# A PEER value stage that takes 32 of its 512 latent tokens by gathered rows, with 16 modulation tiles moved to the input stage

## The chip, the cores and the metric

One core of a Trainium2 chip runs the whole step as one program. The metric is device microseconds of one execution. Times of a kernel are medians of repeated executions; one more execution is taken with the hardware profiler, and all rows below come from that one.

## The reference

Two trunk layers over 128 prompt tokens and 512 latent tokens of 1024 features. Each layer is a mixer and then PEER, a product-key mixture of 16,384 experts. For every token 8 heads pick 16 experts each (128 picks, `idx`) with softmax gates `gsm`. What matters here, cut from the reference:

```
ue = u_tab[idx]
act = jax.nn.gelu(jnp.einsum('td,thkd->thk', xb, ue))
ve = v_tab[idx]
return jnp.einsum('thk,thkd->td', (gsm * act).astype(ve.dtype), ve)
```

The result is multiplied by one of six rows of adaLN modulation and added to the token. That modulation is `silu(c) @ w_mod + b_mod`, 6,144 columns a layer, 48 tiles of 128.

## The kernel before

All data is fp32. A product runs as three fp32r matmuls of split operands (high x high, high x low, low x high), so every weight tile is loaded, split into `w_hi` and `w_lo`, and used three times. Tokens lie in the free dimension as columns 0 to 127 (prompt) and 128 to 639 (latent), features in the partitions.

PEER is dense for the latents. In the **input stage** of a layer, 128 chunks of `u` (128 experts by 1024 features) are multiplied with all tokens: per chunk 24 matmuls of 512 latent columns (`latent_steps`), and per four chunks 24 matmuls for the prompt (`prompt_steps`). ScalarE applies gelu and stores the activations to DRAM (`act_s`). Meanwhile VectorE does the routing (top 16 of keys, then of pairs, `route`), and GpSimd scatters the latents' gates into a zeroed dense table `gate_d`, one indirect DMA for each of 4 tiles x 128 picks (`scatter_gates`). In the **value stage** each of 128 chunks of `v` is multiplied with the product `p` of activations and gates: for a chunk, `form` multiplies a loaded pair `ag` of 512 columns (activations, gates), ScalarE and VectorE split it into `p_his` and `p_los`, `low_v` makes the low part of the weights, and TensorE runs `value_step` for 8 feature tiles (`dt`) with three matmuls each: 24 matmuls of 512 columns a chunk, 3,072 a layer. All 8 sums stay in PSUM over the whole stage, one bank each (`v_bank`). There are 8 slots for weights and for `p`, and 4 for `ag`. Loops run over 16 bodies of 8 chunks.

The prompt's 128 tokens are not dense in the value stage: for pick number k of all 128 tokens, GpSimd gathers 128 rows of `v` (`fetch_row`, 8 buffers `found`) and 128 activations (`fetch_act`), and VectorE adds row times gate times activation to `total` (`parts`, `add_row`), one pick per chunk. At the end of the stage the last four chunks are taken feature tile by feature tile; after the fourth, TensorE transposes `total` into two freed PSUM banks, and VectorE adds the sums to `x` (`ADDS`).

What sets the order: every engine runs its own program, written out by hand, and waits on counting semaphores. SyncE issues all big loads in one queue. It reloads a weight slot when TensorE has finished the chunk 8 earlier (`v_done`; in the input stage groups of four by `made_p`). The modulation tiles that later stages need are computed on VectorE beside PEER in layer 0: `modulate_u` takes one tile (two multiply-and-sum operations over 1024 elements, `L1795`) beside each of the input-stage chunks 112 to 127 (`MODS_AT = 14 * SPLIT`), then 8 more behind chunk 127; `modulate_v` takes 32 further tiles in the value stage, two a body, from two buffers. After the routing and the last `modulate_u` VectorE makes `where_i`, the row numbers of the prompt's picks, on which GpSimd's `values_of` waits.

Of the kernel before, what the change touches and what calls it, by code (L numbers as in the profile page):

```python
# [77 lines left out]
def build(nc, a):  # L78
# [3 lines left out]
    with ctx:  # L82
# [23 lines left out]

        BY_DVE = 10
# [23 lines left out]
        sink = sb("sink", [P, NH])  # L131
        conv_w = sb("conv_w", [P, 4, 3])
# [89 lines left out]
        p_out = [at("p_out0", [P, 512], mask_at), at("p_out1", [P, 512], rope_at + 2048)]  # L222
        l_out = [at(f"l_out{i}", [P, NL_TOK], a_out_at + 2048 * i) for i in range(2)]
        gate_d = [nc.dram_tensor(f"gate_d{l}", (SPOTS + NL_TOK * PICKS, 1), F, kind="Internal").ap() for l in range(2)]
        gate_rows = [t[0:SPOTS].rearrange("(c p t) o -> c p (t o)", c=NKEY, p=P) for t in gate_d]
        act_p = [nc.dram_tensor(f"act_p{l}", (NKEY * P * NP_TOK, 1), F, kind="Internal").ap() for l in range(2)]
# [48 lines left out]
        y_ready, y_out = sem("y_ready"), sem("y_out")  # L275
        block = ctx.enter_context(nc.Block())

        N_CONST, N_CONST1 = 10, 5
        MODS_U = 16
        MODS_AT = 14 * SPLIT  # L280
# [113 lines left out]
        def _(sp):  # L394
# [15 lines left out]
            for l in range(2):  # L410
# [60 lines left out]
                def load_ag(c, u):  # L471
                    if not (isinstance(c, int) and c < 4):
                        sp.wait_ge(p_lo, NKEY * l + c - 3)
                    for w, rows in enumerate((a["act_s"][l, bass.ds(c, 1), :, P:T], gate_rows[l][bass.ds(c, 1)])):
                        sp.dma_start(ag[:, u % 4, w], rows.rearrange("o p n -> (o p) n")).then_inc(ag_in[u % 4], 16)
# [15 lines left out]
                for u in range(GROUP, SPLIT):  # L491
                    load_ag(u, u)
                    if l == 0 and u < GROUP + 2:
                        sp.dma_start(w_mod_v[u - GROUP][:], a["w_mod"][1, MODS_U + u - GROUP])\
                          .then_inc(mod_v_in[u - GROUP], 16)
                with sp.Fori(1, BODIES) as i:
                    for u in range(SPLIT):
# [3 lines left out]
                        if l == 0 and u in (0, 4):  # L501
                            sp.wait_ge(mod_v_used, 2 * i + u // 4 - 1)
# [1627 lines left out]
```

## Time and profile before

| | us |
|---|---|
| runs: median of 3 (lowest, highest) | 4231.42 (4229.95, 4235.04) |
| the profiled execution | 4233.31 |
| its span, first to last instruction | 4231.5 |
| busy: TensorE | 4083.5 (97%) |
| busy: VectorE | 2841.0 (67%) |
| busy: GpSimd | 2218.1 (52%) |
| busy: ScalarE | 1221.0 (29%) |

The value stage of layer 0 runs from about 1398 to 2099 us of the span, that of layer 1 from about 3514 to 4213 us. Busy is the union of an engine's instructions; matmuls overlap, so the spacing of their starts and not their length is what one costs. A row of the chain of waits tells which engine the end hangs on, a row of stretches how busy each engine and the DMA were in one stage.

### The profile page before, as it was taken

What the parts mean: (1) busy time and instruction counts of PE and PEld (TensorE: products, weight loads), DVE (VectorE), ACT (ScalarE), POOL (GpSimd) and SP (SyncE); (2) the same over time, 40 slices, a digit from 0 to 9 for tenths busy, and PEclk for the clock granted to TensorE, in tenths of its full rate; (3) what the DMA queues carried; (4) which work ended last, traced back from release to release, by engine and by line L of the source; (5) the groups of instructions that cost most, each with busy time, mean ns of one, the idle gap of its engine ahead of it and who ended that gap; (6) DMA issues with size and microseconds to landing.
All of it is one profiled execution on the core that took longest, in us unless ns stands there. A gap on an engine that the chain in (4) does not pass through costs nothing.

```text
span 4231.5 us, 57020 instructions
## 1 busy us (share of the span) xinstructions
PE 4083.5 (97%) x19676; PEld 3440.7 (81%) x19676; DVE 2841.0 (67%) x5039; ACT 1221.0 (29%) x1744; POOL 2218.1 (52%) x1784
## 2 busy tenths in 40 slices
PE   7988999999999999999898889999999999999998
PEld 6768988888888788888796689888888888888886
DVE  7877896998125897878634448969981116666665
ACT  2332012232322232333233420122322223333332
POOL 3324447777777554445331134477777755444441
PEclk9989999999999999999999999999999999999999
DMA  5743223333345998888514512333333339888883
GB/s 206 274 175 105 66 107 130 127 129 127 129 143 192 362 350 315 313 313 312 184 54 146 219 65 66 107 130 127 127 129 127 129 120 343 294 290 290 290 287 135
DMA packets 336774, 796.94 MB, mean 188 GB/s; under 512 B 71424, under 2 KB 73184, under 8 KB 336128
## 3 DMA queue, kind: packets, MB, share of 16 engines
q1 hardware_dynamic: 175248, 500.38, 33.4%
q10 hardware_dynamic: 83568, 159.94, 10.2%
q0 software_dynamic: 77824, 134.97, 9.7%
q8 instruction: 67, 1.10, 0.1%
q14 instruction: 67, 0.55, 0.0%
HBM read 640.67 MB, written 154.42 MB: 188 GB/s over the span
## 4 chain that ended last, share of the span: by engine, by line
PE 91%; DVE 5%; DMA 1%; ACT 1%; issue 1%; SPq 0%; POOL 0%; DVEq 0%; ACTq 0%; POOLq 0%
PE acc L605 15%; PE acc L607 15%; PE acc L606 15%; PE aux L887 5%; PE acc L889 5%; PE acc L888 5%; PE aux L888 5%; PE acc L887 5%; PE aux L889 5%; PE acc L842 3%; PE acc L844 3%; PE acc L843 3%; PE aux L812 1%; PE aux L770 1%; DVE unread L1472 1%
## 5 line engine op out<-in xcount | busy, mean ns | idle before, releaser
L574 POOL DMA_INDIRECT gate_d<-gate_v,spot_i x1024 | 1140.3, 1114 | 371.1 <-issue 341.8
L605 PE MATMUL acc<-a_hi,w_hi 128*128 128x512 f32 (+1 forms) x3248 | 1182.8, 364 | 35.0 <-DVE a_lo L1445 30.6
L606 PE MATMUL acc<-a_lo,w_hi 128*128 128x512 f32 (+1 forms) x3248 | 1171.2, 361 | 0.0
L607 PE MATMUL acc<-a_hi,w_lo 128*128 128x512 f32 (+1 forms) x3248 | 1171.1, 361 | 0.0
L605 PEld LDWEIGHTS acc<-a_hi,w_hi 128*128 128x128 f32 x3248 | 613.9, 189 | 130.0 <-issue 48.2
L606 PEld LDWEIGHTS acc<-a_lo,w_hi 128*128 128x128 f32 x3248 | 613.8, 189 | 80.9 <-issue 1.0
L607 PEld LDWEIGHTS acc<-a_hi,w_lo 128*128 128x128 f32 x3248 | 613.2, 189 | 80.1
L1680 DVE TENSOR_TENSOR w_lo<-w_in,w_hi 128x1024 fp32r<-128x1024 f32 x224 | 273.1, 1229 | 573.3 <-ACT w_hi L1213 569.9
L541 POOL DMA_INDIRECT found<-in_v,where_i x256 | 321.1, 1254 | 510.6 <-DVE total L1867 415.1
L1846 DVE TENSOR_TENSOR w_lo<-w_in,w_hi 128x1024 fp32r<-128x1024 f32 x256 | 312.8, 1223 | 223.5 <-ACT w_hi L1252 221.4
L522 POOL CAST w_hi<-w_in 128x1024 fp32r<-128x1024 f32 (+1 forms) x89 | 98.9, 1111 | 664.1 <-DMA w_in<-in_wq 228.4
L547 POOL DMA_INDIRECT pick_act<-act_p,where_i x256 | 319.2, 1247 | 208.7 <-DVE part_now L1853 120.4
L1196 ACT ACTIVATE l_out<-acc 128x512 f32<-128x512 f32 x256 | 153.4, 599 | 879.9 <-PE acc L607 879.6
L887 PE MATMUL aux<-p_his,w_hi 128*128 128x512 f32 x1024 | 398.6, 389 | 6.0 <-DVE p_los L1827 4.0
L887 PE MATMUL acc<-p_his,w_hi 128*128 128x512 f32 x1024 | 398.5, 389 | 0.0
L889 PE MATMUL aux<-p_his,w_lo 128*128 128x512 f32 x1024 | 398.4, 389 | 0.0
L888 PE MATMUL aux<-p_los,w_hi 128*128 128x512 f32 x1024 | 398.4, 389 | 0.0
L888 PE MATMUL acc<-p_los,w_hi 128*128 128x512 f32 x1024 | 398.4, 389 | 0.0
L889 PE MATMUL acc<-p_his,w_lo 128*128 128x512 f32 x1024 | 398.4, 389 | 0.0
L1252 ACT ACTIVATE w_hi<-w_in 128x1024 fp32r<-128x1024 f32 x256 | 270.3, 1057 | 275.1 <-DMA w_in<-in_v 272.6
L1261 ACT ACTIVATE p_his<-ag 128x512 fp32r<-128x512 f32 x256 | 162.1, 633 | 645.0 <-DVE ag L1821 634.2
L1867 DVE SCALAR_TENSOR_TENSOR total<-found,part_now,total 128x1024 f32<-128x1024 f32 x254 | 326.4, 1285 | 11.0 <-DVE part_now L1853 9.8
(275 smaller groups left out, 5991.4 us busy)
## 6 DMA issues: line engine op xcount, KB each, us to landing
w_in<-in_u SPq DMA_DIRECT2D x256, 512.0 KB, 5.1
w_in<-in_v SPq DMA_DIRECT2D x256, 512.0 KB, 4.9
gate_d<-zeros ACTq DMA_DIRECT2D x32, 2048.0 KB, 7.5
act_s<-l_out ACTq DMA_DIRECT2D x256, 256.0 KB
ag<-act_s SPq DMA_DIRECT2D x256, 256.0 KB, 4.8
ag<-gate_d SPq DMA_DIRECT2D x256, 256.0 KB, 5.7
w_in<-in_in SPq DMA_DIRECT2D x32, 512.0 KB, 7.7
w_in<-in_wq SPq DMA_DIRECT2D x32, 512.0 KB, 3.5
```

The costliest lines, as they stand in the source:

```text
L541: pool.indirect_dma_start(found[:, k % FOUND, :], None, rows_of_v, bass.IndirectOffsetOnAxis(ap=where_i[:, 0, k:k + 1], axis=0))\
L547: pool.indirect_dma_start(pick_act[:, k:k + 1], None, act_p[l], bass.IndirectOffsetOnAxis(ap=where_i[:, 1, k:k + 1], axis=0))\
L574: pool.indirect_dma_start(gate_d[l], bass.IndirectOffsetOnAxis(ap=spot_i[:, n, k:k + 1], axis=0), gate_v[:, n, k:k + 1], None).then_inc(sp ...
L605: pe.matmul(out, wh, hi[:, k, n], start=(k == 0), stop=False)
L606: pe.matmul(out, wh, lo[:, k, n], start=False, stop=False)
L607: return pe.matmul(out, wl, hi[:, k, n], start=False, stop=(k == kt - 1))
L887: pe.matmul(v_bank(dt), wh, p_his[:, u, :], start=start, stop=False)
L888: pe.matmul(v_bank(dt), wh, p_los[:, u, :], start=False, stop=False)
L889: return pe.matmul(v_bank(dt), wl, p_his[:, u, :], start=False, stop=stop)
L1680: dve.tensor_tensor(w_lo[:, c % SPLIT, :], landing(c % SPLIT), w_hi[:, c % SPLIT, :].bitcast(F), ALU.subtract).then_inc(lo_v, 1)
L1846: dve.tensor_tensor(w_lo[:, slot, :], landing(slot), w_hi[:, slot, :].bitcast(F), ALU.subtract).then_inc(lo_v, 1)
L1867: dve.scalar_tensor_tensor(total[:], found[:, u, :], part_now[:, u:u + 1], total[:], ALU.mult, ALU.add).then_inc(added, 1)
```

## The change

In both layers the last 32 latent tokens (32 of tile 4, `RW = 32`) are taken out of the dense product of the value stage: matmuls, `form`, `p_his`, `p_los` and the loads of `ag` have 480 columns (`NV`). The 32 tokens' 128 picks each are taken by rows: four groups of 32 partitions hold picks 0 to 31, 32 to 63, 64 to 95 and 96 to 127 of the same 32 tokens, so 32 indirect loads of 128 rows (`found_r`, one buffer) and 32 of 128 activations (`act_r`) cover them. VectorE adds them to `total_r` (two halves of 512), two a body (`add_rest`). After the transposes of `total`, eight matmuls against `same_token` (a 128 x 32 matrix of ones where the token is the same) sum the four groups and turn the result into PSUM, and VectorE adds eight 128 x 32 pieces to `x`. The latents' activations go to a DRAM tensor of their own, `act_d`, of which 512 columns are stored contiguously, so that the gather can address them. The input stage and the scatter of gates still cover all 512 latents.

Before that, SyncE waits for the picks of the routing (`rest_ready`) ahead of the load of input chunk 88, and moves picks and gates of the 32 tokens to the four groups with 8 small DMAs.

The modulation tiles: `modulate_u` now starts beside input chunk 88 and takes 40 tiles, one a chunk, with none behind chunk 127; `modulate_v` takes 16 tiles, one a body, from one buffer.

```
-        MODS_U = 16
-        MODS_AT = 14 * SPLIT
+        MODS_U = 32
+        MODS_AT = 11 * SPLIT
...
-                with sp.Fori(1, MODS_AT // SPLIT if l == 0 else BODIES) as i:
+                with sp.Fori(1, MODS_AT // SPLIT) as i:
                     for u in range(SPLIT):
                         load_inputs(i, u)
+                sp.wait_ge(rest_ready, l + 1)
+                for g in range(GROUPS):
+                    rows = slice(RW * g, RW * g + RW)
+                    sp.dma_start(where_r[rows], pick_ri[P - RW:P, :, rows]).then_inc(rest_moved, 16)
+                    sp.dma_start(gate_r[rows], picks[P - RW:P, 2, NT - 1, rows]).then_inc(rest_moved, 16)
+                if l:
+                    with sp.Fori(MODS_AT // SPLIT, BODIES) as i:
+                        for u in range(SPLIT):
+                            load_inputs(i, u)
...
-                        load_modulation(c - MODS_AT + 4)
-                    for t in range(NKEY - MODS_AT + 4, MODS_LATE + MODS_U):
-                        load_modulation(t)
+                        if c - MODS_AT + 4 < MODS_LATE + MODS_U:
+                            load_modulation(c - MODS_AT + 4)
...
+                pool.wait_ge(rest_moved, 32 * GROUPS * (l + 1))
                 for k in range(FOUND):
                     fetch_row(l, k)
...
                     if k >= FOUND:
                         fetch_row(l, k)
+                    if k % 4 == 1 and k > FOUND:
+                        fetch_rest(l, (k - FOUND) // 4)
+                for e in range(RW - 2, RW):
+                    fetch_rest(l, e)
+
+            def fetch_rest(l, e):
...
+                pool.wait_ge(rest_added, (RW + 1) * l + 1 + e)
+                pool.indirect_dma_start(act_r[:, e:e + 1], None, act_d[l],
+                                        bass.IndirectOffsetOnAxis(ap=where_r[:, 1, e:e + 1], axis=0))\
+                    .then_inc(rest_act, 16)
+                pool.indirect_dma_start(found_r[:], None, rows_of_v,
+                                        bass.IndirectOffsetOnAxis(ap=where_r[:, 0, e:e + 1], axis=0))\
+                    .then_inc(rest_row, 16)
...
-                    pe.matmul(v_bank(dt), wh, p_his[:, u, :], start=start, stop=False)
...
+                    out, hi, lo = v_bank(dt)[:, 0:NV], p_his[:, u, 0:NV], p_los[:, u, 0:NV]
+                    pe.matmul(out, wh, hi, start=start, stop=False)
...
                         mm.then_inc(total_turned, 1)
+                        pe.wait_ge(rest_half, (RW + 1) * (l + 1))
+                        pe.wait_ge(rest_added, (RW + 1) * (l + 1))
+                        pe.wait_ge(v_taken, 16 * l + 3)
+                        for k in range(KD):
+                            mm = pe.matmul(v_bank(2)[:, k * RW:(k + 1) * RW],
+                                           total_r[k // 4][:, k % 4 * P:(k % 4 + 1) * P], same_token[:],
+                                           start=True, stop=True)
+                        mm.then_inc(rest_summed, 1)
...
-                    for t in range(NKEY - MODS_AT, MODS_LATE + MODS_U):
-                        modulate_u(t)
...
+                def add_rest(e):
+
+                    dve.wait_ge(rest_act, 16 * (RW * l + 1) + 16 * e)
+                    dve.wait_ge(rest_row, 16 * (RW * l + 1) + 16 * e)
+                    n = (RW + 1) * l + 1 + e
+                    dve.wait_ge(rest_added, n)
+                    dve.tensor_tensor(part_r[:], act_r[:, bass.ds(e, 1)], gate_r[:, bass.ds(e, 1)], ALU.mult)\
+                       .then_inc(rest_part, 1)
+                    dve.wait_ge(rest_part, RW * l + 1 + e)
+                    dve.wait_ge(rest_half, n)
+                    for h, done in enumerate((rest_half, rest_added)):
+                        dve.scalar_tensor_tensor(total_r[h][:], found_r[:, h * 512:(h + 1) * 512], part_r[:, 0:1],
+                                                 total_r[h][:], ALU.mult, ALU.add).then_inc(done, 1)
+
                 def body(i):
                     for u in range(SPLIT):
                         half = (u // 4 + 1) % 2
                         chunk(i, u, i - 1 if half else i, half)
+                        if u % 4 == 1:
+                            add_rest(2 * i - 2 + u // 4)
...
+                add_rest(RW - 2)
                 parts(BODIES - 1, 1)
                 for j in range(4):
                     add_row(BODIES - 1, 1, j)
+                add_rest(RW - 1)
...
-                        dve.wait_ge(total_turned, l + 1)
+                        if k == 0:
+                            dve.wait_ge(total_turned, l + 1)
+                            dve.wait_ge(rest_summed, l + 1)
+                        note(dve.scalar_tensor_tensor(x[:, k, P + NV:T], v_bank(2)[:, k * RW:(k + 1) * RW],
+                                                      mod[:, l, 40 + k, 1:2], x[:, k, P + NV:T], ALU.mult, ALU.add))
```

The order in three places. On GpSimd, at the start of the value stage, before (`found` are rows for the prompt, `pick_act` activations):

```order
L541 DMA found<-in_v,where_i 128x1024 x8
L547 DMA pick_act<-act_p,where_i 128x1 x12
L541 DMA found<-in_v,where_i 128x1024 x4
L547 DMA pick_act<-act_p,where_i 128x1 x4
L541 DMA found<-in_v,where_i 128x1024 x4
L547 DMA pick_act<-act_p,where_i 128x1 x4
```

and with the change, where a row load and an activation load of the 32 tokens come in after every fourth row:

```order
L567 DMA found<-in_v,where_i 128x1024 x8
L573 DMA pick_act<-act_p,where_i 128x1 x12
L567 DMA found<-in_v,where_i 128x1024 x2
L605 DMA act_r<-act_d,where_r 128x1
L608 DMA found_r<-in_v,where_r 128x1024
L567 DMA found<-in_v,where_i 128x1024 x2
L573 DMA pick_act<-act_p,where_i 128x1 x4
```

So GpSimd's queue gets two indirect DMAs for every eight that it had. On VectorE, two chunks of a body of the value stage with the change (`ag` is `form`, `total` is `add_row`, `p_los` and `w_lo` are the low parts, `total_r` is `add_rest`):

```order
L1881 TENSOR_TENSOR ag<-ag 128x480
L1926 SCALAR_TENSOR_TENSOR total<-found,part_now,total 128x1024
L1886 REGISTER_ALU
L1887 TENSOR_TENSOR p_los<-ag,p_his 128x480
L1904 REGISTER_ALU
L1905 TENSOR_TENSOR w_lo<-w_in,w_hi 128x1024
L1948 ISA
L1952 ISA
L1952 TENSOR_TENSOR part_r<-act_r,gate_r 128x1
L1957 SCALAR_TENSOR_TENSOR total_r_158<-found_r,part_r,total_r_158 128x512
L1957 SCALAR_TENSOR_TENSOR total_r_159<-found_r,part_r,total_r_159 128x512
L1881 TENSOR_TENSOR ag<-ag 128x480
```

The three `part_r` and `total_r` operations stand behind the low parts of every fourth chunk; before, `ag` of the next chunk followed at once. On TensorE, after the fourth feature tile of a layer's last four chunks (`aux` and `acc` are PSUM banks):

```order
L934 MATMUL aux<-p_his,w_lo 128x480
L971 MATMUL aux<-ident,total 128x128 x8
L978 MATMUL aux<-same_token,total_r_158 128x32 x4
L978 MATMUL aux<-same_token,total_r_159 128x32 x4
L932 MATMUL acc<-p_his,w_hi 128x480
```

Before, the first matmul of the fifth feature tile came directly behind the eight transposes.

## Rows read from the trace of the kernel before

**Rows 1.** The page: the chain that ended last, by engine.
```profile
PE 91%; DVE 5%; DMA 1%; ACT 1%; issue 1%; SPq 0%; POOL 0%; DVEq 0%; ACTq 0%; POOLq 0%
```

**Rows 2.** Stretches: us, busy PE, PEld, DVE, ACT, POOL, clock, DMA share, GB/s.
```profile
1259.00:1394.00 135.00, 135.00 (x598) 111.77 (x597) 77.47 (x118) 36.69 (x46) 85.19 (x68) 1.00 0.64 212
1440.00:1510.00 70.00, 70.00 (x310) 57.95 (x310) 68.66 (x90) 25.39 (x33) 44.90 (x33) 1.00 1.04 395
1650.20:1997.40 347.20, 347.20 (x1533) 287.51 (x1532) 275.40 (x353) 105.97 (x128) 159.64 (x128) 1.00 0.88 313
3700.00:4047.20 347.20, 347.20 (x1533) 287.49 (x1532) 234.88 (x271) 108.18 (x128) 156.93 (x128) 1.00 0.82 289
```

**Rows 3.** Timeline of TensorE, value stage of layer 0: start us, us long, what.
```profile
1699.81 0.39 PE L888 MATMUL aux<-p_los,w_hi 128*128 128x512 f32 x1
...
1701.85 0.39 PE L888 MATMUL aux<-p_los,w_hi 128*128 128x512 f32 x1
```

**Rows 4.** Timeline of TensorE, layer 0's projection to keys, 320 columns a matmul.
```profile
429.78 0.31 PE L607 MATMUL acc<-a_hi,w_lo 128*128 128x320 f32 x1
...
432.86 0.31 PE L607 MATMUL acc<-a_hi,w_lo 128*128 128x320 f32 x1
```

**Rows 5.** Timeline of TensorE's weight loads in the same stretch.
```profile
430.07 0.19 PEld L607 LDWEIGHTS acc<-a_hi,w_lo 128*128 128x128 f32 x1
```

**Rows 6.** Timeline of TensorE where value stages start, in brackets idle before, and releaser.
```profile
1397.98 0.50 PE L887 MATMUL aux<-p_his,w_hi 128*128 128x512 f32 x1 [2.52 <-DVE p_los L1827]
1422.06 0.47 PE L887 MATMUL aux<-p_his,w_hi 128*128 128x512 f32 x1 [2.02 <-DVE w_lo L1846]
3513.57 0.50 PE L887 MATMUL aux<-p_his,w_hi 128*128 128x512 f32 x1 [1.51 <-DVE p_los L1827]
```

**Rows 7.** Timeline of VectorE between input and value stage of layer 0.
```profile
1371.32 1.22 DVE L1795 CUSTOM_DVE_ANT_0 unread_u<-w_mod_u,c_all 128x1024 f32<-128x1024 f32 x1
...
1392.24 0.29 DVE L1814 CAST where_i<-where 128x256 uint32<-128x256 f32 x1
...
1419.22 0.16 DVE L1853 TENSOR_TENSOR part_now<-pick_act,picks 128x4 f32<-128x4 f32 x1 [5.10 <-DMA pick_act<-act_p,where_i]
```

**Rows 8.** Timeline of VectorE, end of layer 0's routing.
```profile
1072.58 0.29 DVE L1745 TENSOR_TENSOR picks<-picks,best 128x128 f32<-128x128 f32 x1
```

**Rows 9.** Timeline of SyncE's queue: loads of input chunks 88 to 91 of layer 0.
```profile
1096.45 2.03 SPq L442 DMA_DIRECT2D w_in<-in_u  x4
```

**Rows 10.** Groups by line, VectorE, 1650.2 to 1997.4: busy us, mean ns | idle before.
```profile
L1867 DVE SCALAR_TENSOR_TENSOR total<-found,part_now,total 128x1024 f32<-128x1024 f32 x65 | 83.6, 1286 | 2.0 <-DVE part_now L1853 1.7
L1821 DVE TENSOR_TENSOR ag<-ag 128x512 f32<-128x512 f32 x64 | 44.0, 688 | 28.7 <-DMA ag<-gate_d 28.5
```

**Rows 11.** The same view, GpSimd.
```profile
L547 POOL DMA_INDIRECT pick_act<-act_p,where_i x64 | 81.5, 1274 | 43.4 <-DVE part_now L1853 28.8 <-issue 14.6
L541 POOL DMA_INDIRECT found<-in_v,where_i x64 | 78.8, 1232 | 145.5 <-DVE total L1867 134.6 <-issue 10.9
```

**Rows 12.** DMA queues, 3650 to 4050 us: packets, MB, share of 16 engines.
```profile
q1 hardware_dynamic: 31654, 77.00, 53.2%
q0 software_dynamic: 12832, 38.25, 29.0%
```

**Rows 13.** The tile `where_i`: time from issue to landing of GpSimd's indirect loads.
```profile
DMA to landing us min/median/max: 4.1/6.7/15.5
```

**Rows 14.** Timeline of VectorE, end of layer 0's value stage.
```profile
2060.38 5.45 DVE L1867 SCALAR_TENSOR_TENSOR total<-found,part_now,total 128x1024 f32<-128x1024 f32 x4
2097.81 0.75 DVE L1913 SCALAR_TENSOR_TENSOR x<-acc,mod,x 128x512 f32<-128x512 f32 x1 [0.98 <-PE acc L889]
2098.48 0.34 DVE L1913 SCALAR_TENSOR_TENSOR x<-aux,mod,x 128x128 f32<-128x128 f32 x1
```

**Rows 15.** Timeline of TensorE: matmuls of 2 columns early on; transposes of layer 0's `total`.
```profile
37.31 4.63 PE L729 MATMUL aux<-c_cols,w_mod 128*128 128x2 f32 x41
...
2085.83 1.04 PE L926 MATMUL aux<-ident,total 128*128 128x128 f32 x8
```

More of the change, by code:

```diff
@@ L131, in build @@
         sink = sb("sink", [P, NH])
+        same_token = sb("same_token", [P, RW])
         conv_w = sb("conv_w", [P, 4, 3])
@@ L222, in build @@
         p_out = [at("p_out0", [P, 512], mask_at), at("p_out1", [P, 512], rope_at + 2048)]
+        found_r = at("found_r", [P, D], work + 49152)
+        total_r = [at("total_r0", [P, 512], mask_at), at("total_r1", [P, 512], rope_at + 2048)]
+        pick_r = at("pick_r", [P, 2, PICKS], work + 46080)
+        pick_ri = at("pick_ri", [P, 2, PICKS], work + 47104, U32)
+        where_r = at("where_r", [P, 2, RW], work + 53248, U32)
+        gate_r = at("gate_r", [P, RW], work + 53504)
+        act_r = at("act_r", [P, RW], work + 53632)
+        part_r = at("part_r", [P, 1], work + 53760)
         l_out = [at(f"l_out{i}", [P, NL_TOK], a_out_at + 2048 * i) for i in range(2)]
@@ L225, in build @@
         gate_rows = [t[0:SPOTS].rearrange("(c p t) o -> c p (t o)", c=NKEY, p=P) for t in gate_d]
+        act_d = [nc.dram_tensor(f"act_d{l}", (SPOTS, 1), F, kind="Internal").ap() for l in range(2)]
+        act_rows = [t.rearrange("(c p t) o -> c p (t o)", c=NKEY, p=P) for t in act_d]
         act_p = [nc.dram_tensor(f"act_p{l}", (NKEY * P * NP_TOK, 1), F, kind="Internal").ap() for l in range(2)]
@@ L566, in values_of @@
                         fetch_row(l, k)
+                    if k % 4 == 1 and k > FOUND:
[3 more added lines that the diff above has]
+            def fetch_rest(l, e):
+                if e == 0:
+                    for s in range(2):
+                        pool.wait_ge(a_st[s], 16 * A_ALL[s] * (l + 1))
+                pool.wait_ge(rest_added, (RW + 1) * l + 1 + e)
[5 more added lines that the diff above has]
+                    .then_inc(rest_row, 16)
             def scatter_gates(l):
@@ L1508, in _ @@
             step(dve.tensor_copy(iota_b[:], iota[:]))
+            step(dve.tensor_reduce(same_token[:], ident[:].rearrange("p (g t) -> p t g", t=RW), AX.X, ALU.add))
             step(dve.tensor_tensor_reduce(out=unread[:, 0:P], in0=ident[:], in1=iota[:], scale=float(NKEY * P),
@@ L1789, in route @@
                 share(0)
+                step(dve.scalar_tensor_tensor(pick_r[:, 0, :], picks[:, 1, NT - 1, :], float(P),
+                                              picks[:, 0, NT - 1, :], ALU.mult, ALU.add))
+                step(dve.tensor_scalar(pick_r[:, 1, :], pick_r[:, 0, :], float(NL_TOK), tokens[:, NT - 2:NT - 1],
+                                       ALU.mult, ALU.add))
+                if l:
+                    step(dve.tensor_scalar(pick_r[:, 0, :], pick_r[:, 0, :], float(NKEY * P), None, ALU.add))
+                dve.tensor_copy(pick_ri[:], pick_r[:]).then_inc(rest_ready, 1)
                 def modulate_u(t):
@@ L1897, in experts @@
                     chunk(0, u, 0, 0, first=True)
+                for k, done in enumerate((rest_half, rest_added)):
+                    dve.wait_ge(p_st[k], 16 * FOURS // 2 * (l + 1))
+                    dve.memset(total_r[k][:], 0.0).then_inc(done, 1)
                 with dve.Fori(1, BODIES) as i:
                     body(i)
+                add_rest(RW - 2)
                 parts(BODIES - 1, 1)
```

59 lines of the change are left out of this document (32 added, 27 removed).

## The prediction

> **What bounds the kernel now.** I read the chain of waits first: TensorE carries 91% of it [rows 1]. Then stretches of the two value stages, away from their ends: in 347.2 us TensorE is busy for all 347.2, at a granted clock of 1.00, the upper of its two levels (2.4 GHz) [rows 2]. Beside it VectorE is busy for 79% (layer 0) and 68% (layer 1), GpSimd for 46%, and the DMA engines for 88% and 82%. So the value stage is a row of matmuls without holes, and the reader should ask two things: what one matmul costs, and which of the helpers would be the next bound. A matmul costs the spacing of starts: 9 steps in 1701.85 - 1699.81 = 2.04 us, 0.2267 us at 512 columns [rows 3]. At 320 columns 21 steps take 3.08 us, 0.1467 us [rows 4]. The slope is 0.0800 / 192 = 0.417 ns a column, the rest (13 ns) is fixed. TensorE stood idle at the start of the stages only: 2.52 and 2.02 us in layer 0, 1.51 us in layer 1 [rows 6].
>
> How far ahead is the feed? The last low part of layer 0 is made before 2060.38, when VectorE turns to its last four rows [rows 14]. TensorE ends the fourth feature tile of the last four chunks at 2085.83 [rows 15], four times 12 x 0.2267 = 10.9 us after it began them: 2074.9. All four were ready 14.6 us before; in plain order chunk 127 would come three chunks of 5.44 us later, so the lead is about 31 us of the 8 x 5.44 = 43.5 us that 8 slots allow. A body of 8 chunks is those 43.5 us.
>
> **The matmuls.** 2 layers x 128 chunks x 24 = 6,144 matmuls lose 32 columns: 32 x 0.417 = 13.3 ns each, new spacing 0.2133 us. **-81.9 us**, all of it on the chain as long as the feed keeps up. A body becomes 41.0 us. About this slope the Trainium skill ("TensorE: Matmul & The Clock Gate", section "Back-to-back issue gap") has another figure: in a stream of weight loads and matmuls it gives 81 ns at 128 columns and 131 ns at 512, 0.13 ns a column. By it the term would be 25.6 us (an estimate from that page) and the time 4208.6 us. The two rows decide: the same kinds of instruction, 320 and 512 columns, stand 80 ns apart and not 25.
>
> **What the feed must do in a body.** Four helpers:
> - VectorE, layer 0: 275.4 / 8 = 34.4 us a body [rows 2]. It loses one modulation tile, 2 x 1.22 + some 0.3 = 2.75 us [rows 7], and a sixteenth of 16 operations of 0.688 us, 0.7 us [rows 10]. It gains two `add_rest`, each one tiny operation (0.16 us, as `part_now` [rows 7]) and two sums of 512: between half of the 1024-wide sum, 0.64 us [rows 10], and the 0.75 us of the 512-wide one that reads PSUM [rows 14]. I take 0.66, the first, since both read SBUF: 1.5 us each, 3.0 us a body. Result 34.0 of 41.0 us. Layer 1: 234.9 / 8 = 29.4, -0.7, +3.0 = 31.7 us.
> - GpSimd: 8 rows and 8 activations cost 160 / 8 = 20.0 us a body; 4 more loads at 1.23 to 1.27 us [rows 11] make 25.0 us.
> - DMA, layer 0: 0.88 x 43.5 = 38.3 us a body. Two row loads of 0.52 MB with their activation loads cost what GpSimd's queue takes for a pair, 29.0% of 400 us over 74 pairs = 1.57 us each, +3.1 us [rows 12]. The other queue moves 77.00 MB in 212.8 us [rows 12], 362 GB/s: 0.26 MB less of `ag`, -0.7 us, one tile of 0.52 MB less, -1.45 us. Result 39.2 of 41.0 us, 0.96; layer 1: 0.82 x 43.5 + 3.1 - 0.7 = 38.1, 0.93. At the start of layer 0's stage the share stood at 1.04 for 70 us, with 395 GB/s [rows 2]; the new body needs 13.9 MB in 41.0 us, 339 GB/s. It fits, with little room: this is the nearest bound.
> - ScalarE has 31% of its time in use and gets less.
>
> So TensorE stays the bound, with a lead of about 28 us of the 41.
>
> **The new waits.** `found_r` is one buffer: GpSimd fetches row set e only when VectorE has added e-1, and behind that wait stand the prompt's row loads. VectorE in turn waits for the landing. The turn is fetch (two issues of 1.3 us and gaps, 3.1 us), landing (median 6.7 us), and adding (1.5 us): 11.3 us. It may take four chunks, 20.5 us. The prompt's rows behind it have 8 buffers, 41 us. At the first set, the zeroing of `total_r` stands ahead, two chunks before the first `add_rest`; landing may make VectorE wait there some 4 us, when TensorE is about 5 us behind it. Cost: nothing, with the lead as cover; without it, up to 4 us once a layer.
>
> **SyncE's queue.** Its wait for the picks ends after the last step of routing, 1072.58 + 0.29 us [rows 8] and four small operations of about 0.3 us: 1074. Eight small issues of at most 0.5 us end at 1078. The next load in the queue, of chunk 88, was due at 1096.45 [rows 9], as it waits for TensorE: 18 us to spare, nothing lost. GpSimd waits for these moves only when it is through with the scatter. From there on 24 more tiles sit beside input chunks 88 to 111, and the 16 more tile loads pass through this queue between chunk loads. VectorE then works 1.2 + 2.5 = 3.7 us of a chunk's 6.8 us. That is what chunks 112 to 127 did already, and TensorE was busy for 135.0 of 135.0 us there [rows 2]. Cost: nothing.
>
> **The start of layer 0's value stage.** From 1371.32 VectorE works off the 8 tiles behind chunk 127, until `where_i` at 1392.24 [rows 7]. Row loads, activation loads and weights then land together, and VectorE gets the first activations only at 1419.22; hence 2.52 us and 2.02 us of idle TensorE. Without the 8 tiles this start is like that of layer 1, which idles once, for 1.51 us [rows 6]: **-3.0 us** (0 if the landings stay as late).
>
> **The end of each stage.** Between the transposes and the fifth feature tile TensorE now does eight fp32 matmuls of 32 columns. Nearest row: 41 of 2 columns in 4.63 us, 0.113 us each; that row counts two for each matmul in the program, so 16, 1.8 us. Below, the eight transposes took 1.04 us; above, 16 at twice the time (the lower clock level), 3.6 us [rows 15]. I take 1.8. VectorE adds a 128 x 32 piece before the last prompt piece: a 128 x 128 one takes 0.34 us [rows 14], I take 0.2. Twice 2.0: **+4.0 us**. The wait on the last row set hides: VectorE ends its rows some 15 us ahead of the first sum.
>
> **Sum**, against the profiled execution: 4233.3 - 81.9 - 3.0 + 4.0 = 4152.4 us. The median of the runs lies 1.9 us below that execution, so I forecast **4150.5 us**.
>
> **Rivals.**
> - *DMA becomes the bound.* For it: 0.96 of the body by my count, and landings grow with load. Against it: 395 GB/s over 70 us. If steady traffic could not pass 324 GB/s, the bodies would take 13.9 / 0.324 = 42.9 us in layer 0 and, at 312 GB/s for its 13.4 MB, 42.9 us in layer 1: 2 x 15 x 1.9 = 57 us, less a lead of 28 us used up in each layer, so near +2 by this alone, and about +28 if the lead is never built in layer 0, where the stage starts with a full DMA. 4152 to 4180. Chance 0.09.
> - *The single buffer paces the stage: slower.* Upper ends: landing 15.5 us [rows 13], four activation loads of 1.27 us ahead of the fetch, 3.1 us and 1.5 us: 25.2 us a turn, against 20.5. Then 2 x 31 x 4.7 = 291 us, less two leads of 28: 4387 us. It decides from (81.9 + 56) / 62 = 2.2 us over 20.5, so 22.7 us a turn. Against it: every one of the loads would have to land at the longest time; the median turn is 11.3 us. Chance 0.03.
> - *Weight loads, not columns, set the pace in this stage.* A weight load shows 0.19 us under each matmul; were it the floor, the spacing would stay at 0.2267 and the time be 4232.5 us, no change. Against it: at 320 columns the same loads of 0.19 us stand under starts 0.147 us apart [rows 4, 5]. Chance 0.02, the in-between slope of the Trainium skill included.
> - Something unseen in the input stage or the routing: 0.02.
>
> **Numbers.** Forecast 0.84. The range, 4145 to 4172 us: below, the end of the stages at 1.1 us each (4148.7) and the spread of the runs before (1.5 us down, 3.6 up); above, 3.6 us there, no gain at the start (4157), and most of the DMA rival. Not within it: the slower rival, the weight loads, the worst of the DMA. Some 0.2% is what a measurement of this kernel tells from no change: faster by more than that 0.95, within 0.02, slower 0.03.
>
> **What would show it.** Right: spacing 0.213 us in both value stages, each some 41 us shorter; TensorE still without idle in the middle; one idle of about 1.5 us at the start of layer 0's stage; VectorE at 83% and DMA at 0.96 there; no wait on `found_r` or `act_r` that TensorE inherits; 1.8 us of matmuls on `same_token`. Wrong: idle TensorE that ends with `w_lo` or `p_los` all along the stage (DMA or the single buffer), spacing above 0.215 us, or idle around input chunk 88.

## The result and the profile after

| | before | after |
|---|---|---|
| runs: median (lowest, highest), us | 4233.23 (4229.95, 4236.06), 4 runs | 4182.14 (4180.19, 4183.36), 4 runs |
| the profiled execution, us (its span) | 4233.31 (4231.5) | 4181.42 (4179.5) |

After over before is 0.988, 95% interval 0.9868 to 0.9892: faster by 51 us. The direction was right, but the time is 32 us above the forecast of 4150.5 us and outside the range. Two views say at once that a term was missed. The first is the chain of waits of the page, where TensorE had 91% before and GpSimd 0% [rows 1]:

```profile
PE 71%; POOL 15%; DVE 6%; issue 5%; DMA 1%; ACT 1%; SPq 0%; DVEq 0%; ACTq 0%; POOLq 0%
```

GpSimd has 15% of it, all of it the scatter of gates (`gate_d`, L618). The second view is the timeline of TensorE at the end of layer 0's input stage and the start of its value stage (start us, us long, what; in brackets idle before and what ended it):

```profile
1390.67 0.39 PE L888 MATMUL acc<-w_lo,a_hi 128*128 128x512 f32 x1
1402.35 0.77 PE L932 MATMUL aux<-p_his,w_hi 128*128 128x480 f32 x1 [11.29 <-DVE p_los L1887]
1426.33 0.45 PE L932 MATMUL aux<-p_his,w_hi 128*128 128x480 f32 x1 [0.93 <-DVE w_lo L1905]
...
3492.44 0.49 PE L932 MATMUL aux<-p_his,w_hi 128*128 128x480 f32 x1 [1.45 <-DVE p_los L1887]
```

TensorE idles 11.29 us where it idled 2.52 [rows 6]; 4.4 us of this come from an input stage that ended earlier in this execution (1391.06, before 1395.46), for a reason that stays open. One step back on VectorE, one on SyncE's queue and one on GpSimd lead to what it waits for:

```profile
1400.31 0.66 DVE L1881 TENSOR_TENSOR ag<-ag 128x480 f32<-128x480 f32 x1 [16.76 <-DMA ag<-gate_d]
```

```profile
1397.51 0.43 SPq L501 DMA_DIRECT2D ag<-gate_d  x1
```

```profile
1394.78 0.96 POOL L618 DMA_INDIRECT gate_d<-gate_v,spot_i  x1 [0.30 <-issue]
1397.86 0.97 POOL L567 DMA_INDIRECT found<-in_v,where_i  x1 [2.11 <-DMA gate_d<-gate_v,spot_i]
```

The first loads of gates can only go out when the last scatter has landed, and that one was issued at 1394.78. In the kernel before it was issued at 1365.48, followed by a long wait for `where_i` (the next two rows), and the first gates were loaded 19.3 us later (the third row, SyncE's queue):

```profile
1365.48 1.57 POOL L574 DMA_INDIRECT gate_d<-gate_v,spot_i  x1 [0.30 <-issue]
1392.81 1.70 POOL L541 DMA_INDIRECT found<-in_v,where_i  x1 [25.76 <-DVE where_i L1814]
```

```profile
1384.76 0.50 SPq L475 DMA_DIRECT2D ag<-gate_d  x1
```

The first value matmul started 7.57 us after the last scatter's issue here; in three more runs below whose scatter ended late it was 7.67 to 7.81 us. So for a start at 1397.98, as before, the last scatter had to be issued by about 1390.4 (an estimate from these rows): 24.9 us of slack before the change. It came 29.3 us later, and the start 4.37 us later.

The stretches that answer to [rows 2] (us, then busy PE, PEld, DVE, ACT, POOL, clock, DMA share, GB/s); the second is the start of layer 0's value stage, the last two are the middles of both value stages:

```profile
1259.00:1394.00 135.00, 132.06 (x583) 109.11 (x581) 60.45 (x87) 36.20 (x45) 106.26 (x86) 1.00 0.50 171
1394.00:1440.00 46.00, 36.72 (x159) 31.44 (x160) 23.23 (x33) 9.24 (x13) 25.04 (x24) 0.86 0.85 310
1440.00:1510.00 70.00, 70.00 (x325) 60.63 (x324) 66.89 (x91) 24.91 (x32) 56.41 (x42) 1.00 1.03 402
1650.20:1950.00 299.80, 299.80 (x1385) 259.65 (x1385) 249.65 (x327) 94.15 (x117) 185.31 (x146) 1.00 0.91 332
3600.00:3950.00 350.00, 350.00 (x1617) 303.11 (x1616) 270.36 (x341) 110.78 (x137) 203.74 (x174) 1.00 0.91 326
```

In the middle of both value stages TensorE has no hole. So there the time depends on the spacing alone, in the timeline of TensorE:

```profile
1699.63 0.38 PE L933 MATMUL acc<-p_los,w_hi 128*128 128x480 f32 x1
1699.85 0.38 PE L934 MATMUL acc<-p_his,w_lo 128*128 128x480 f32 x1
...
1702.23 0.38 PE L933 MATMUL aux<-p_los,w_hi 128*128 128x480 f32 x1
```

Twelve steps take 2.60 us: 0.2167 us each, where the forecast had 0.2133. From the first to the last start of a value matmul the stages took 699.40 and 697.13 us before, 671.32 and 668.16 after. The account of the two spans (the parts between and behind the stages hold mostly work that the change does not touch): start of layer 0's stage +4.37 (1397.98 to 1402.35), the stages -28.08 and -28.97, between them +2.59, behind the second -1.90, together -51.99 of the -52.0 us.

### The profile page after: what moved, and what is told of

Same layout as the page of the kernel before. It is cut to its first block, busy times and chain, and to the rows that moved or that the text cites. A ratio compares the mean times of both kernels' runs of the same rounds, so it can differ in the third digit from the quotient of the medians.

```text
span 4179.5 us, 57329 instructions
## 1 busy us (share of the span) xinstructions
PE 4022.1 (96%) x19708; PEld 3443.6 (82%) x19708; DVE 2924.0 (70%) x5243; ACT 1206.8 (29%) x1744; POOL 2407.5 (58%) x1912
## 4 chain that ended last, share of the span: by engine, by line
PE 71%; POOL 15%; DVE 6%; issue 5%; DMA 1%; ACT 1%; SPq 0%; DVEq 0%; ACTq 0%; POOLq 0%
POOL gate_d L618 15%; PE acc L649 10%; PE acc L651 10%; PE acc L650 10%; PE aux L932 5%; PE acc L932 5%; PE acc L933 5%; PE aux L934 5%; PE acc L934 5%; PE aux L933 5%; PE acc L888 1%; PE acc L887 1%; PE acc L886 1%; PE aux L856 1%; DVE unread L1525 1%
## 5 line engine op out<-in xcount | busy, mean ns | idle before, releaser
L618 POOL DMA_INDIRECT gate_d<-gate_v,spot_i x1024 | 1176.3, 1149 | 369.5 <-issue 340.2
L573 POOL DMA_INDIRECT pick_act<-act_p,where_i x256 | 309.5, 1209 | 213.7 <-DVE part_now L1912 121.0
L567 POOL DMA_INDIRECT found<-in_v,where_i x256 | 312.0, 1219 | 174.2 <-DVE total L1926 93.6
L932 PE MATMUL aux<-p_his,w_hi 128*128 128x480 f32 x1024 | 388.8, 380 | 13.7 <-DVE p_los L1887 12.7
L933 PE MATMUL aux<-p_los,w_hi 128*128 128x480 f32 x1024 | 388.2, 379 | 0.0
L934 PE MATMUL aux<-p_his,w_lo 128*128 128x480 f32 x1024 | 388.1, 379 | 0.0
L932 PE MATMUL acc<-p_his,w_hi 128*128 128x480 f32 x1024 | 387.6, 379 | 0.0
L933 PE MATMUL acc<-p_los,w_hi 128*128 128x480 f32 x1024 | 387.6, 379 | 0.0
L934 PE MATMUL acc<-p_his,w_lo 128*128 128x480 f32 x1024 | 387.5, 378 | 0.0
L1314 ACT ACTIVATE p_his<-ag 128x480 fp32r<-128x480 f32 x256 | 155.3, 606 | 710.3 <-DVE ag L1881 680.4
```

Source lines behind the costliest of these rows:

```text
L567: pool.indirect_dma_start(found[:, k % FOUND, :], None, rows_of_v, bass.IndirectOffsetOnAxis(ap=where_i[:, 0, k:k + 1], axis=0))\
L573: pool.indirect_dma_start(pick_act[:, k:k + 1], None, act_p[l], bass.IndirectOffsetOnAxis(ap=where_i[:, 1, k:k + 1], axis=0))\
L618: pool.indirect_dma_start(gate_d[l], bass.IndirectOffsetOnAxis(ap=spot_i[:, n, k:k + 1], axis=0), gate_v[:, n, k:k + 1], None).then_inc(sp ...
L932: pe.matmul(out, wh, hi, start=start, stop=False)
L933: pe.matmul(out, wh, lo, start=False, stop=False)
L934: return pe.matmul(out, wl, hi, start=False, stop=stop)
```

## The experiments

### Is it the width, or the new traffic?

Theory A: 0.2167 us is what 480 columns cost, whatever runs beside them. Theory B: 480 columns would cost 0.2133, and the 32 gathers a layer slow TensorE down. The first kernel is the one before with eight widths in the eight slots of a body; the columns above a width are left out.

```
+                    nv = 512 if start else (512, 504, 496, 488, 480, 472, 464, 448)[u]
+                    out, hi, lo = v_bank(dt)[:, 0:nv], p_his[:, u, 0:nv], p_los[:, u, 0:nv]
...
```

> The kernel before, but the value matmuls of the eight chunks of a body take 512, 504, 496, 488, 480, 472, 464 and 448 columns (the first of a stage 512); the latents' sums lack those columns of these chunks. Everything else is as before, so the feed is not changed. Theory A (the 480-column matmul itself is dearer than the line through 320 and 512): the mean spacing at 480 is 0.2167 us here too, as in the changed kernel, and the other widths show from where; at 448, a multiple of 64 as 320 and 512 are, 0.200 us. Theory B (the gathers or their sums slow TensorE in the changed kernel): every width lies on the line, 0.2133 us at 480, 0.2200 at 496, 0.2233 at 504.

The second has `(512, 440, 512, 416, 512, 384, 496, 352)`.

> As the other ruler, with 512, 440, 512, 416, 512, 384, 496 and 352 columns in the eight chunks of a body; the latents' sums lack the rest. Theory A: 384 (a multiple of 64) on the line, 0.1733 us; 440, 416 and 352 (odd multiples of 8, 32, 32) some 3 ns above their line values of 0.1967, 0.1867 and 0.1600 us. Theory B: all on the line.

Mean spacing of starts, from 721 to 736 spacings each (512 columns in the second: 2,176); in the last column the spacing in cycles of 2.4 GHz (the granted clock is 1.00), less the columns:

| columns | us | cycles over the columns |
|---|---|---|
| 352 | 0.1599 | 32 |
| 384 | 0.1745 | 35 |
| 416 | 0.1866 | 32 |
| 440 | 0.1998 | 39 |
| 448 | 0.2027 | 38 |
| 464 | 0.2088 | 37 |
| 472 | 0.2132 | 40 |
| 480 | 0.2169 | 41 |
| 488 | 0.2200 | 40 |
| 496 | 0.2233, 0.2235 | 40 |
| 504 | 0.2268 | 40 |
| 512 | 0.2278, 0.2272 | 35, 33 |

Both rulers leave out sums that the result needs, and each was profiled in one execution; only their spacings are used. In the timeline of the second kernel, 22 steps at 416 columns take 4.11 us, and at 440 columns 4.40 us:

```profile
1694.92 0.35 PE L890 MATMUL aux<-p_los,w_hi 128*128 128x416 f32 x1
...
1699.03 0.35 PE L891 MATMUL acc<-p_his,w_lo 128*128 128x416 f32 x1
...
1723.70 0.36 PE L890 MATMUL aux<-p_los,w_hi 128*128 128x440 f32 x1
...
1728.10 0.36 PE L891 MATMUL acc<-p_his,w_lo 128*128 128x440 f32 x1
```

No gather of the 32 tokens runs here and 480 columns cost 0.2169 us: B falls. The line through 320 and 512 columns holds within 3 cycles at 352, 384, 416 and 512; from 440 to 504 a matmul costs 5 to 9 cycles more than on it. The first 8 columns taken off 512 bring almost nothing. Of theory A's guesses on which widths are dear only that for 440 came true: 448, a multiple of 64, was to lie on the line and costs 0.2027 us instead of 0.2000; 384 was to lie on it and costs 1 ns more, and 416 and 352 were to lie 3 ns above it and lie on it. What makes the step stays open. The third kernel sets all to 480 and leaves the last 32 latents without a PEER result:

```
+                    nv = 480
...
```

> The kernel before with the value matmuls of all chunks at 480 columns and nothing in their place: the PEER result of the last 32 latents is left out; loads, splits and modulation are as before. Theory A: mean spacing 0.2167 us, so 6144 x 10.0 ns = 61 us less than before, near 4172 us. Theory B: spacing 0.2133 us, 82 us less, near 4151 us. Idle times at the start of layer 0's value stage as before, 2.5 and about 2 to 3 us.

4172.88 us (4163.51 to 4173.9, 4 runs), ratio 0.985, interval 0.983 to 0.9871: 61 us from 4234.15, and 6,144 x (0.2267 - 0.2167) is 61.4. A holds; the width alone is worth 61 us, not 82.

### Do the moved tiles delay the scatter?

Theory C: the multiply-and-sums of the 24 more tiles beside chunks 88 to 111 stretch GpSimd's scatter, and so TensorE starts late. Theory D: they cost nothing there, and the late start comes from the rest of the change. The kernel before with the move of the tiles alone:

```
-        MODS_U = 16
-        MODS_AT = 14 * SPLIT
+        MODS_U = 32
+        MODS_AT = 11 * SPLIT
...
-                    for t in range(NKEY - MODS_AT, MODS_LATE + MODS_U):
-                        modulate_u(t)
...
```

> The kernel before with the moved modulation tiles alone: 40 tiles beside input chunks 88 to 127, 16 in the value stage; all 512 latents dense. Theory C (each multiply-and-sum of a tile holds up GpSimd's scatter by about half a microsecond to one, 48 more of them make it end some 29 us later, after TensorE is through with the input stage): the last scatter issues near 1395 us, the value stage starts after about 11 us of idle TensorE, and the time is about 6 to 10 us over before, near 4241 us. Theory D (the late start comes from the 32 tokens: SyncE's wait, its 8 moves, GpSimd's wait for them): the scatter ends as before near 1366 us, the start idles 1.5 us as in layer 1, the time is near 4230 us.

4241.38 us (10 runs), ratio 1.0022, interval 1.0012 to 1.0031. The last scatter is issued at 1398.97, and TensorE starts so:

```profile
1406.78 0.80 PE L885 MATMUL aux<-p_his,w_hi 128*128 128x512 f32 x1 [10.28 <-DVE p_los L1823]
```

C holds: by itself the move makes the kernel 7 us slower. The other way round, the changed kernel with the tiles where they were (16 beside chunks 112 to 127, 8 behind, 32 in the value stage):

```
-        MODS_U = 32
-        MODS_AT = 11 * SPLIT
+        MODS_U = 16
+        MODS_AT = 14 * SPLIT
...
```

> The changed kernel with the modulation tiles as before: 16 beside input chunks 112 to 127 and 8 behind, 32 in the value stage, two a body. Theory C (the moved tiles beside the scatter make the late start): scatter ends near 1366 us, idle at the start of layer 0's value stage 2.5 us and at most 3 us at its fifth chunk, against 11.7 us; the time is about 8 us under the changed kernel, near 4174 us, if the DMA carries two tiles a body as well (by my count 0.98 of a body of 41.6 us). Theory D (the 32 tokens' moves and waits make it): idle near 11 us again, time near 4182 us. If the DMA does not carry it, TensorE waits for weights along layer 0's stage and the time is over 4180 us.

4178.19 us (4172.76 to 4185.44, 4 runs), ratio 0.9876, interval 0.986 to 0.9893; idle 2.56 and 3.05 us at the start, as before the change. SyncE's wait and its moves are in it, and cost nothing that shows. Its last scatter is issued at 1367.90. Its median lies 5.3 us above that of 480 columns alone, but its four runs spread over 12.7 us, so this is no measure of the 4.0 us that the forecast put on the end of the stages; nor can this kernel be told from the changed one by its time. That the late start goes with the tiles is shown by the traces. A middle way takes 24 tiles beside chunks 104 to 127, none behind, and leaves 32 in the value stage:

```
-        MODS_U = 32
-        MODS_AT = 11 * SPLIT
+        MODS_U = 16
+        MODS_AT = 13 * SPLIT
...
```

> As rests_alone, but modulation starts beside input chunk 104, so that 24 tiles stand one a chunk and none behind chunk 127. Theory C: the 16 added operations beside the scatter delay its end by about 10 us, to 1376 us, still before TensorE is through; the picks' row numbers are there 20 us earlier than with tiles behind chunk 127, so the stage starts as in layer 1, after 1.5 us: 3 us under rests_alone, near 4171 us. Theory D: no difference to rests_alone in the start.

4172.42 us (4168.53 to 4173.75, 4 runs), ratio 0.9854, interval 0.9838 to 0.9871; one idle of 1.44 us, last scatter at 1379.75. No run of it is as slow as any of the changed kernel, which ran again beside it:

> The changed kernel itself beside the two, on the same chip: near 4182 us, 11.7 us idle at the start of layer 0's value stage.

4182.84 us (4182.52 to 4187.39, 4 runs), ratio 0.9885, interval 0.9869 to 0.9902. This time TensorE idles 8.87 and 2.25 us; the last scatter is issued at 1396.97 and the first value matmul starts at 1404.64.

### Which part of a tile holds the scatter?

A tile is a load of 0.52 MB and two multiply-and-sums. Theory E says the operations, F the loads. The kernel before, with two operations a chunk more on data that lies in SBUF, through a helper (`step`) that waits for each before going on:

```
+                    if l == 0 and 88 <= c < MODS_AT:
+                        for h in range(2):
+                            step(dve.tensor_tensor_reduce(out=unread_u[:, h, :], in0=c_all[:, 0, :],
+                                                          in1=c_all[:, 1, :], scale=1.0, scalar=0.0, op0=ALU.mult,
+                                                          op1=ALU.add, accum_out=mod_v[:, 2, h:h + 1]))
```

> The kernel before, with two multiply-and-sum operations a chunk added on VectorE beside input chunks 88 to 111 of layer 0, over data that lies in SBUF; no load is added. (Left out: nothing that the result needs; the added sums are not used.) Theory E, VectorE's multiply-and-sums hold up GpSimd's scatter: scatter DMAs that start beside one take some 1.9 us instead of 0.96, and the last scatter is issued near 1395 us of the span instead of 1365.5, TensorE's idle at the start of layer 0's value stage is 8 to 14 us instead of 2.5, time 4238 to 4246 us. Theory F, the added tile loads (DMA traffic) hold it up: the last scatter stays near 1366 us, the idle near 2.5 us, time within 3 us of the kernel before.

And with 24 loads more, without an operation:

```
+                        sp.dma_start(w_mod_u[:, c % 4, :], a["w_mod"][1, c - 88]).then_inc(extra_in[c % 4], 16)
...
```

> The kernel before, with 24 loads of a modulation tile (0.52 MB each) added in SyncE's queue beside input chunks 88 to 111 of layer 0; VectorE does nothing more. (Left out: nothing that the result needs; the added loads are not used.) Theory E (VectorE's operations hold up the scatter): the last scatter stays near 1366 us, the idle at the start of the value stage near 2.5 us, time within 3 us of the kernel before. Theory F (the tile loads' traffic holds it up): last scatter near 1395 us, idle 8 to 14 us, time 4238 to 4246 us.

4230.99 and 4233.09 us, ratios 1.0001 (0.9991 to 1.001) and 1.0006 (0.9995 to 1.0016): neither costs time, so that E missed the time and the idle that it foresaw for the operations (2.31 us instead of 8 to 14). GpSimd's groups by line, 1110 to 1390 us (busy us, mean ns | idle before), of the kernel before, then operations, then loads:

```profile
L574 POOL DMA_INDIRECT gate_d<-gate_v,spot_i x176 | 193.7, 1101 | 64.2 <-issue 64.2
```

```profile
L574 POOL DMA_INDIRECT gate_d<-gate_v,spot_i x181 | 209.4, 1157 | 61.2 <-issue 61.2
```

```profile
L582 POOL DMA_INDIRECT gate_d<-gate_v,spot_i x177 | 197.3, 1115 | 65.9 <-issue 65.9
```

The loads move a scatter's mean by 14 ns and the last scatter to 1371.93, 6.5 us later where F foresaw 29: F falls as the main cause; whether a small part is theirs is not shown. The operations move the mean by 56 ns and the last scatter to 1379.34, half of what E foresaw and still ahead of 1390.4, so that no time is lost. The changed kernel shows why it was half. Its GpSimd and VectorE, in the same microseconds:

```profile
1202.24 0.96 POOL L618 DMA_INDIRECT gate_d<-gate_v,spot_i  x1 [0.31 <-issue]
1203.50 1.22 POOL L618 DMA_INDIRECT gate_d<-gate_v,spot_i  x1 [0.30 <-issue]
1205.03 1.97 POOL L618 DMA_INDIRECT gate_d<-gate_v,spot_i  x1 [0.30 <-issue]
```

```profile
1202.66 1.23 DVE L1734 TENSOR_TENSOR w_lo<-w_in,w_hi 128x1024 fp32r<-128x1024 f32 x1 [1.56 <-ACT w_hi L1266]
1203.81 1.22 DVE L1857 CUSTOM_DVE_ANT_0 unread_u<-w_mod_u,c_all 128x1024 f32<-128x1024 f32 x1
...
1204.95 1.22 DVE L1857 CUSTOM_DVE_ANT_0 unread_u<-w_mod_u,c_all 128x1024 f32<-128x1024 f32 x1
```

The scatter of 1203.50 begins while `w_lo` runs, and ends at 1204.72, 0.83 us after `w_lo` ended (1203.89). That of 1205.03 begins 0.08 us into the tile's second operation and ends at 1207.00, 0.83 us after that ended (1206.17). That of 1202.24 began with VectorE idle, and takes its 0.96 although `w_lo` starts 0.42 us later. So a scatter is held by the `w_lo` or tile operation that runs when it begins, until 0.83 us behind its end, and not by one that starts later. This is no matter of three examples. In both layers of this trace 182 scatters began with more than 0.18 us of such an operation still to run. The 166 that began 45 ns or more behind its start all ended 0.83 to 0.84 us behind its end; the 16 that began earlier in it, or at 45 ns, took 0.95 to 0.96 us. Not every operation holds one. The 176 scatters that began beside the routing's `MAX8`, `FIND_INDEX8`, `MATCH_REPLACE8` and `TENSOR_REDUCE` operations, counted in the same way, took 0.95 to 0.98 us, like this one, which ends while the operation still runs (VectorE, then GpSimd):

```profile
869.57 1.59 DVE L1818 TENSOR_REDUCE spot<-same 128x48 f32<-128x768 f32 x1
```

```profile
869.80 0.96 POOL L618 DMA_INDIRECT gate_d<-gate_v,spot_i  x1 [0.30 <-issue]
```

A tile's operations start 1.14 us apart, and scatters 1.264: in the rows above, the second operation starts just ahead of a scatter and costs it 1.01 us. With a wait between them, as in the run above, the operations stand 1.26 us apart, in step with the scatters, and slip in behind their starts. This is theory E2; theory G says that only operations that read the tiles' landing buffer hold a scatter. The run with 48 operations, back to back:

```
+                    if l == 0 and 88 <= c < MODS_AT:
+                        if c > 88:
+                            dve.wait_ge(extra_used, c - 88)
+                        for h in range(2):
+                            ins = dve.tensor_tensor_reduce(out=unread_u[:, h, :], in0=c_all[:, 0, :],
...
+                        ins.then_inc(extra_used, 1)
```

> As the run with 48 added operations, but the two multiply-and-sums of a chunk are issued back to back, without a wait for the first between them, as the modulation tiles issue theirs (starts 1.14 us apart instead of 1.27 us, where a scatter starts every 1.264 us). Theory E2, a scatter DMA issued while a VectorE operation runs is held until it ends, so that the price hangs on how the operations stand to the scatter's starts: 0.7 us an operation as for the tiles' own, last scatter issued at 1390 to 1400 us, TensorE's idle at the start of layer 0's value stage 6 to 14 us, time 4236 to 4246 us. Theory G, only operations that read the tiles' landing buffer hold it up: last scatter near 1379 us, idle near 2.5 us, time within 3 us of the kernel before.

4239.68 us (9 runs), ratio 1.0022, interval 1.0012 to 1.0033. The last scatter is issued at 1400.56 and the mean of one is 1289 ns. TensorE idles 17.15 us, more than foreseen, but the profiled execution is the slowest of the nine (4253.35 us). G falls. And the changed kernel, with the wait added in `modulate_u`:

```
+                        if c == 0:
+                            step(ins)
                     ins.then_inc(mod_u_used, 1)
+                    dve.wait_ge(mod_u_used, t + 1)
```

> The changed kernel whole, with one edit: VectorE waits for the first multiply-and-sum of a modulation tile before it issues the second, and for the second before it goes on, so that their starts lie 1.27 us apart and not 1.14 us. Theory E2: fewer scatters are held, some 0.3 to 0.45 us an operation instead of 0.68, last scatter issued at 1366 to 1380 us instead of 1394.8, idle at the start of the value stage 1.5 to 5 us instead of 11.3, time 4171 to 4177 us. Theory G: last scatter near 1395 us, idle near 11 us, 4180 to 4185 us.

4171.8 us (4169.56 to 4172.64, 4 runs), ratio 0.9856, interval 0.984 to 0.9873. The chain of waits, the last scatter, GpSimd's group over 1110 to 1390 us, and the start of the stage:

```profile
PE 92%; DVE 5%; ACT 1%; issue 1%; DMA 1%; SPq 0%; DVEq 0%; ACTq 0%
```

```profile
1358.76 0.96 POOL L618 DMA_INDIRECT gate_d<-gate_v,spot_i  x1 [0.30 <-issue]
```

```profile
L618 POOL DMA_INDIRECT gate_d<-gate_v,spot_i x175 | 184.1, 1052 | 65.7 <-issue 65.7
```

```profile
1397.88 0.49 PE L932 MATMUL aux<-p_his,w_hi 128*128 128x480 f32 x1 [1.45 <-DVE p_los L1890]
```

In the same microseconds as above, a scatter now begins 0.05 us ahead of a tile's second operation, and is not held:

```profile
1205.38 0.96 POOL L618 DMA_INDIRECT gate_d<-gate_v,spot_i  x1 [0.30 <-issue]
```

```profile
1205.43 1.23 DVE L1857 CUSTOM_DVE_ANT_0 unread_u<-w_mod_u,c_all 128x1024 f32<-128x1024 f32 x1
```

Counted over the last 200 scatters of layer 0, by the operation that ran when a scatter began (in brackets, what these scatters took beyond 0.96 us each, in sum):

| | before | changed | spaced |
|---|---|---|---|
| beside a tile's operation | 14 (14.3 us) | 40 (39.7 us) | 2 (1.0 us) |
| beside `w_lo` | 40 (11.5 us) | 41 (18.3 us) | 38 (17.3 us) |

The same work, with the same tiles at the same chunks, ends its scatter 36 us earlier than the changed kernel; GpSimd is off the chain again, and the first value stage is 668.15 us long. E2 holds, and the scatter ended earlier than it foresaw. This kernel and the middle way above are the fastest of the study, 10 us ahead of the changed kernel; they can't be told apart. The changed kernel was not run beside this one, but none of its eight runs on two other chips is under 4180.19 us, and none of the four here is over 4172.64.

## Why the prediction was right and where it was wrong

- **"The matmuls", -81.9 us: the size was wrong.** The mechanism was right, since TensorE has no hole in the middle of either stage and the saving is on the chain. But the slope was read between 320 and 512 columns, and 480 does not lie on that line: 0.2167 us, so 6,144 x 0.0100 = 61.4 us, 20.5 us less. A price at one size was interpolated between two far ones, with nothing in the trace near it. The rule of the Trainium skill ("TensorE: Matmul & The Clock Gate", section "Back-to-back issue gap") that was weighed against it, 0.13 ns a column, would have given 4 ns a matmul; measured are 10. The 4208.6 us that the prediction gives for that rule count from the profiled execution; from the same base as the forecast they would be 4206.8.
- **"From there on 24 more tiles sit beside input chunks 88 to 111 ... Cost: nothing": wrong.** The step counted VectorE's time in a chunk and found TensorE busy in all of chunks 112 to 127. It did not look at the third engine beside the tiles. In the stretch before, GpSimd was busy 85.19 of 135 us [rows 2], now 106.26: the scatter, whose end bounds the first load of gates. Its slack, 24.9 us by the estimate above, was never named, and 29.3 us of delay (1365.48 to 1394.78) used it up. The Trainium skill ("SBUF — State Buffer", section "Who interferes with whom") says that a VectorE instruction with two inputs in SBUF contends with a GpSimd instruction that reads SBUF. The rows agree: `w_lo` and the multiply-and-sums have two such inputs, and scatters that begin beside them last until 0.83 us behind their end. Two inputs alone do not decide, though: `FIND_INDEX8` and `MATCH_REPLACE8` name two input tiles each (`best` and `cand`, or `top_v` and `scores`) and held none of 53 scatters. The section goes on to infer that an operation of two tensors leaves the making of a DMA's descriptors, its list of transfers, alone; this scatter is a DMA that GpSimd issues, and it is held. Whether the making of its descriptors is held or the reading of its row numbers, the rows do not show.
- **"The start of layer 0's value stage", -3.0 us: wrong in the changed kernel, for the same reason.** TensorE started 4.37 us later than before, and after an idle of 11.29 us it ran its first matmuls partly at the lower clock level (1.2 GHz): the mean granted is 0.61 over 1402 to 1408 us and 0.86 over 1394 to 1440 us. That stage is 3.2 us longer than in the kernel with spaced operations (671.32 to 668.15 us; 0.93 us of it is the second idle). With the scatter in time, one idle of 1.45 us is left of 2.52 and 2.02: -3.1 us, as predicted. The sum of the forecast with the measured spacing, 4150.5 + 20.5 = 4171.0 us, is near that kernel's 4171.8; runs of one kernel differ by some 3 us, so that it comes this near is in part luck. Of the 29.0 us by which the profiled execution of the changed kernel missed its 4152.4, then, 20.5 are the spacing and some 8 this start.
- **"What the feed must do in a body": right.** VectorE 249.65 / 299.80 = 83% in layer 0, as said, and 77% in layer 1; GpSimd 62% (61% foreseen); DMA 0.91 in both (0.96 and 0.93 foreseen). The longer body, 41.6 us and not 41.0, explains 0.01 of that; the rest of layer 0's difference stays open. At the start the DMA engines passed 402 GB/s. The DMA rival did not come.
- **"The new waits": right.** VectorE's waits and GpSimd's, 1440 to 2062 us (us in total, times, longest us):

```profile
DVE part_r L1952 <- DMA found_r<-in_v,where_r: 4.4, 3, 2.5
```

```profile
POOL act_r L605 <- DVE total_r L1957: 43.6, 13, 12.7
```

  GpSimd waits for the one buffer, VectorE hardly, TensorE not at all. A half sum took 0.75 us instead of the 0.66 taken, without effect.
- **"The end of each stage", 1.8 us of matmuls on `same_token`: right**, in the timeline of TensorE and that of VectorE:

```profile
2060.81 1.03 PE L971 MATMUL aux<-ident,total 128*128 128x128 f32 x8
2061.68 1.87 PE L978 MATMUL aux<-same_token,total_r 128*128 128x32 f32 x16
2063.39 0.47 PE L932 MATMUL acc<-p_his,w_hi 128*128 128x480 f32 x1
```

```profile
2074.71 0.24 DVE L1994 SCALAR_TENSOR_TENSOR x<-aux,mod,x 128x32 f32<-128x32 f32 x1
```

- **The rivals.** None of the three named ones was what happened: the DMA engines and the single buffer did not pace TensorE, and the spacing did not stay at 0.2267 us. The measured slope lies between the two that the prediction had, a case that it put into the 0.02 of the weight loads; the late start fell into "something unseen in the input stage", which had 0.02. The prediction named "spacing above 0.215 us" as what would prove it wrong, and that came true.

## What to carry to other kernels

Before work is put beside a stage, look at every engine that is busy there, and at what its end releases: a busy TensorE in the same stretch proves nothing about a third engine whose result is due only at the next stage. Where an engine's cost depends on what another does at the moment of its start, the order and spacing of operations can matter more than their number: two waits a tile, which shift a tile's second operation by 0.12 us, were worth 10 us here. A price per column should be measured at the size that will be used; one run with several sizes in the slots of a loop gives them all.

## What the runs showed of the hardware that was not expected

- Spacing of these matmuls at a granted clock of 1.00 is columns + 32 cycles of 2.4 GHz at 320, 352 and 416 columns and at 512 in the kernel before (33 and 35 in the two rulers), and about columns + 40 from 472 to 504 (0.2268 us at 504, 0.2267 to 0.2278 at 512). Why was not found.
- An indirect DMA of GpSimd, the scatter of gates, takes 0.96 us to issue. One that begins while `w_lo` or a tile's multiply-and-sum runs (VectorE, 128x1024 fp32, two operands in SBUF) lasts until 0.83 us behind the end of that operation, in layer 0 beside these up to 2.01 us; beside `MAX8`, `FIND_INDEX8`, `MATCH_REPLACE8` and `TENSOR_REDUCE` it takes its 0.96 us.
- So the price hangs on the timing: scatters that began beside a tile's operation cost 39.7 us over the 80 operations of the changed kernel, 0.50 us each; with the waits it was 1.0 us over the 76 operations ahead of the last scatter. What `w_lo` costs the scatter hardly changed (18.3 and 17.3 us).
